# Up projection of a ConvGLU layer: eight column pairs by seven products of quadrants in place of eight (Strassen)

## The reference, cut to what matters

```python
u = jnp.einsum('bsd,df->bsf', x, w_up[l])
u_gate, u_val = jnp.split(u, 2, axis=-1)
a = jax.nn.gelu(causal_depthwise_conv(u_gate, w_conv[l], b_conv[l]), approximate=False) * u_val
ffn = jnp.einsum('bsf,fd->bsd', a, w_down[l])
x = layer_norm(DEEPNORM_ALPHA * x + ffn, ln2_g[l], ln2_b[l])
```

## Time and profile before

| what | value |
|---|---|
| median of 3 runs | 750.19 us (749.51 to 750.6) |
| the profiled execution | 750.42 us |
| its span | 748.6 us, mean granted clock 0.997 |
| PE busy | 736.8 us (98%), 3475 matmuls |
| PEld busy | 615.6 us (82%) |
| DVE, ACT, POOL busy | 361.7, 325.4, 336.5 us |

### The profile page before, as it was taken

The page is one execution under the profiler, slowest core; times in us unless marked ns, Lnnn a source line. Parts: engine busy times, 40 slices in busy tenths (PEclk is TensorE's granted clock), DMA queues, the critical chain, the costliest instruction groups (busy, mean ns, idle before and its releaser), DMA issues.

```text
span 748.6 us, 9524 instructions
## 1 busy us (share of the span) xinstructions
PE 736.8 (98%) x3475; PEld 615.6 (82%) x3475; DVE 361.7 (48%) x551; ACT 325.4 (43%) x439; POOL 336.5 (45%) x244
## 2 busy tenths in 40 slices
PE   9999999999999999999999999999999999999995
PEld 6888888788888888888898888888888888888884
DVE  3339589789789764455642211221221122322567
ACT  4325775775775775661123322333233233423410
POOL 6645343433424444991015454544445452755800
PEclk9999999999999999999999999999999999999998
DMA  8333314214124214670003222232323227232002
GB/s 306 105 113 111 115 57 121 76 57 137 61 84 113 85 57 157 236 252 29 0 2 134 91 92 104 84 112 84 111 85 101 95 91 289 98 112 84 29 28 84
DMA packets 24477, 78.32 MB, mean 105 GB/s; under 512 B 2944, under 2 KB 3328, under 8 KB 24448
## 3 DMA queue, kind: packets, MB, share of 16 engines
...
## 4 chain that ended last, share of the span: by engine, by line
PE 87%; DVE 6%; ACT 2%; issue 2%; DMA 1%; SPq 0%; DVEq 0%; ACTq 0%
PE ps L1035 86%; PE ps L1137 1%; DVE sb_t L847 1%; DMA fx_k<-k_bias_rows 1%; DVE fx_p L838 1%; DVE sb_t L878 1%; DVE sb_k L802 0%; ACT sb_hi L614 0%; DVE fx_p L875 0%; PE ps L1218 0%; DMA w_raw<-w_stream_in 0%; ACT w_hi L497 0%; DVE fx_lo L731 0%; DVE fx_k L731 0%; DVE q_bias_rows L791 0%
## 5 line engine op out<-in xcount | busy, mean ns | idle before, releaser
L430 POOL TENSOR_TENSOR w_lo<-w_raw,w_hi 128x512 fp32r<-128x512 f32 x218 | 292.4, 1363 | 368.5 <-ACT w_hi L497 362.5
L497 ACT ACTIVATE w_hi<-w_raw 128x1024 fp32r<-128x1024 f32 x108 | 114.3, 1058 | 212.4 <-DMA w_raw<-w_stream_in 212.2
L1035 PE MATMUL ps<-x1T_hi,w_hi 128*128 128x512 f32 (+1 forms) x376 | 141.3, 376 | 0.0
L1035 PE MATMUL ps<-x1T_lo,w_hi 128*128 128x512 f32 (+1 forms) x376 | 141.2, 375 | 0.0
L1035 PE MATMUL ps<-x1T_hi,w_lo 128*128 128x512 f32 (+1 forms) x376 | 141.2, 375 | 0.0
L998 DVE SCALAR_TENSOR_TENSOR conv<-ps,col,conv 128x511 f32<-128x511 f32 (+1 forms) x44 | 33.0, 749 | 166.8 <-ACT conv L694 163.8
L1035 PE MATMUL ps<-xT_hi,w_hi 128*128 128x512 f32 x264 | 105.2, 399 | 0.0
L1035 PE MATMUL ps<-xT_lo,w_hi 128*128 128x512 f32 x264 | 102.9, 390 | 0.0
L1035 PE MATMUL ps<-xT_hi,w_lo 128*128 128x512 f32 x256 | 100.0, 391 | 0.0
L1035 PEld LDWEIGHTS ps<-x1T_hi,w_hi 128*128 128x128 f32 x376 | 70.8, 188 | 12.9
L1035 PEld LDWEIGHTS ps<-x1T_lo,w_hi 128*128 128x128 f32 x376 | 70.8, 188 | 12.8
...
## 6 DMA issues: line engine op xcount, KB each, us to landing
w_raw<-w_stream_in SPq DMA_DIRECT2D x109, 512.0 KB, 3.3
...
```

What stands on the lines that cost most here:

```text
L430: lo = nc.gpsimd.tensor_tensor(w_lo[:, slot, cs], w_raw[:, slot, cs], plain(w_hi[:, slot, cs]), ALU.subtract)
L497: nc.scalar.activation(w_hi[:, slot, :], w_raw[:, slot, :], ACT.Copy).then_inc(hi_ready, 1)
L1035: return nc.tensor.matmul(out_, lhs, rhs, start=start, stop=stop, skip_group_check=True)
```

## The change

For f = 5, 7, ..., 19 (`S_FROM` = 2, `S_END` = 10: the odd member of pairs 2 to 9) the two weight blocks are taken as one matrix of 1024 features by 256 columns. It is cut in quadrants (`b11`, `b21` the halves of the gate block, `b12`, `b22` those of the up block), as is the input (512 features by 256 tokens), and the four quadrants of the result are made of seven products by Strassen's rule in place of eight. Each product has 4 x 3 matmuls of 256 columns.

- The sums of quadrants of the input (five, `s_raw`, with high and low parts `s_hi`, `s_lo`) are made once, at the start of the up stage: eleven additions of 1024 elements per partition on DVE, five copies on ACT, five subtractions on DVE.
- The sums of quadrants of the weight (five, `t_raw`) are made anew for each such f by `w_sums`: five additions of 512 elements on DVE, from the raw slots; the high parts by five copies on ACT, the low parts by five subtractions on POOL. Two products take a quadrant of the weight itself; for these ACT makes 512 columns of each block and POOL 512, in place of 1024 each.
- Products are accumulated in PSUM where the rule allows it. The rest is put together by a copy on ACT (`m_two`) and six additions of 256 elements on DVE; PE waits for the first of these (`m25_added`) before its fifth product, since that product overwrites what the addition reads.
- SP loads the next gate block only when the five sums are made. The f of even number and f = 0 to 3, 20, 21 are made as before.

```diff
+S_FROM, S_END = 2, FB // 2 - 1
+N_S = S_END - S_FROM
+T_ORDER = (1, 6, 3, 4, 7)
...
+        GATE_SLOT, UP_SLOT = (N_UP + 2) % 4, (N_UP + 3) % 4
+        C11, C21, C12, C22, M1 = (ps[:, c:c + HALF] for c in (1024, 1024 + HALF, 3 * 512, 5 * 512, 6 * 512))
+        def x_quarter(tile, keys, tokens):
+            return tile[:, 4 * keys:4 * keys + 4, HALF * tokens:HALF * (tokens + 1)]
...
-            with sp.Fori(0, n_loop) as i:
+            assert n_loop == S_END
+            for n in range(N_UP + 4, N_UP + 4 + 4 * S_FROM):
+                load_when_free(n)
+            with sp.Fori(S_FROM, S_END) as i:
                 for j in range(4):
                     sp.wait_ge(block_done, 4 * i + (N_UP + 1 + j))
+                    if j == 2:
+                        sp.wait_ge(t_summed, 5 * i + (5 - 5 * S_FROM))
                     load(4 * i + (N_UP + 4 + j), (N_UP + j) % 4)
...
+            with pool.Fori(S_FROM, S_END) as i:
+                pool.wait_ge(hi_ready, 4 * i + (N_UP + 3))
+                nc.gpsimd.tensor_tensor(w_hi[:, GATE_SLOT, 512:1024], w_raw[:, GATE_SLOT, 0:512],
+                                        plain(w_hi[:, GATE_SLOT, 0:512]), ALU.subtract).then_inc(lo_ready, 1)
+                pool.wait_ge(hi_ready, 4 * i + (N_UP + 4))
+                nc.gpsimd.tensor_tensor(w_hi[:, UP_SLOT, 0:512], w_raw[:, UP_SLOT, 512:1024],
+                                        plain(w_hi[:, UP_SLOT, 512:1024]), ALU.subtract).then_inc(lo_ready, 1)
+                for j, m in enumerate(T_ORDER):
+                    pool.wait_ge(t_hi_done, 5 * i + (j + 1 - 5 * S_FROM))
+                    nc.gpsimd.tensor_tensor(t_lo[m][:], t_raw[m][:], plain(t_hi[m][:]),
+                                            ALU.subtract).then_inc(t_split, 1)
+                for j in range(4, 6):
+                    low(4 * i + (N_UP + j), (N_UP + j) % 4)
...
+            def gated_up(f, j, ready, count):
+                act.wait_ge(ready, count)
+                act.wait_ge(act_ready, f + 1)
+                nc.scalar.activation(conv[:, j, :], bank(2 * j), ACT.Identity,
+                                     bias=col[:, ds(COL_CB + f, 1)],
+                                     scale=col[:, ds(f * CONV_WIDTH + (COL_CW + CONV_WIDTH - 1), 1)]
+                                     ).then_inc(cv_biased, 1)
+                act.wait_ge(cv_done, f + 1)
+                nc.scalar.activation(gelu[:, j, :], conv[:, j, :], ACT.Gelu).then_inc(gelu_done, 1)
+            def plain_up(f):
+                gated_up(f, f % 2, block_done, N_UP + 2 * f + 1)
...
+            def sums_high(ms):
+                for m in ms:
+                    act.wait_ge(s_summed, S_ORDER.index(m) + 1)
+                    nc.scalar.activation(s_hi[m][:], s_raw[m][:], ACT.Copy).then_inc(s_hi_done, 1)
...
+            high_in_order(N_UP + 3)
+            high_in_order(N_UP + 4)
+            sums_high(S_ORDER[:3])
+            plain_up(0)
...
+            with act.Fori(S_FROM, S_END) as i:
+                for g, (slot, own) in enumerate(((GATE_SLOT, slice(0, 512)), (UP_SLOT, slice(512, 1024)))):
+                    n = N_UP + 2 + g
+                    arrived(None, slot, i + n // 4)
+                    act.wait_ge(block_done, 4 * i + (n - 3))
+                    nc.scalar.activation(w_hi[:, slot, own], w_raw[:, slot, own], ACT.Copy).then_inc(hi_ready, 1)
+                for j, m in enumerate(T_ORDER):
+                    act.wait_ge(t_summed, 5 * i + (j + 1 - 5 * S_FROM))
+                    nc.scalar.activation(t_hi[m][:], t_raw[m][:], ACT.Copy).then_inc(t_hi_done, 1)
+                gated_up(2 * i, 0, block_done, 4 * i + (N_UP + 1))
+                act.wait_ge(block_done, 4 * i + (N_UP + 3))
+                nc.scalar.activation(m_two[:], C21, ACT.Copy).then_inc(m2_copied, 1)
+                for j in range(4, 6):
+                    n = N_UP + j
+                    high(None, n % 4, i + n // 4, 4 * i + (n - 3))
+                gated_up(2 * i + 1, 1, gate_done, i + (1 - S_FROM))
+            high_in_order(N_DOWN - 2)
+            high_in_order(N_DOWN - 1)
+            act.wait_ge(m7_done, N_S)
             a_high(0, 0)
             a_high(1, 1)
-            up_pair(FB // 2 - 1)
+            high_in_order(N_DOWN)
+            plain_up(FB - 2)
+            high_in_order(N_DOWN + 1)
+            high_in_order(N_DOWN + 2)
...
+            def times_halves(f, count):
+                dve.wait_ge(gelu_done, f + 1)
+                dve.wait_ge(up_done, count)
+                halves = ps[:, 3 * 512:7 * 512].rearrange("p (t c) -> p t c", t=2)[:, :, 0:HALF]
+                nc.vector.tensor_tensor(aT[:, ds(f, 1), :].rearrange("p o (t c) -> p (o t) c", t=2), halves,
+                                        gelu[:, 1, :].rearrange("p (t c) -> p t c", t=2),
...
+            def x_sum(m):
+                hi = lambda keys, tokens=0: blocks(plain(x_quarter(x1T_hi, keys, tokens)))
+                lo = lambda keys, tokens=0: blocks(plain(x_quarter(x1T_lo, keys, tokens)))
+                whole = blocks(s_raw[m][:])
+                steps = {2: ((turned(0), hi(1, 1), ALU.add), (whole, lo(1, 1), ALU.add)),
+                         5: ((hi(0), hi(1), ALU.add), (whole, lo(0), ALU.add), (whole, lo(1), ALU.add)),
+                         1: ((turned(1), hi(0), ALU.add), (whole, lo(0), ALU.add)),
+                         6: ((turned(0), hi(0), ALU.subtract), (whole, lo(0), ALU.subtract)),
+                         7: ((hi(1), turned(1), ALU.subtract), (whole, lo(1), ALU.add))}
+                for i, (a, b, op) in enumerate(steps[m]):
+                    done = sum(len(steps[n]) - 1 for n in S_ORDER[:S_ORDER.index(m)]) + i
+                    if i > 0:
+                        dve.wait_ge(s_part, done)
+                    nc.vector.tensor_tensor(whole, a, b, op).then_inc(
+                        s_part if i < len(steps[m]) - 1 else s_summed, 1)
+            def x_sum_low(m):
+                dve.wait_ge(s_hi_done, S_ORDER.index(m) + 1)
+                split_lo(s_lo[m][:], s_raw[m][:], s_hi[m][:]).then_inc(s_split, 1)
+            def w_sums(i):
+                for slot in (GATE_SLOT, UP_SLOT):
+                    dve.wait_ge(raw_in[slot], 16 * i + (16 * ((N_UP + 2 + (slot == UP_SLOT)) // 4) + 16))
+                b11, b21 = (w_raw[:, GATE_SLOT, 512 * k:512 * (k + 1)] for k in range(2))
+                b12, b22 = (w_raw[:, UP_SLOT, 512 * k:512 * (k + 1)] for k in range(2))
+                for m, a, b, op in ((1, b11, b22, ALU.add), (6, b11, b12, ALU.add), (3, b12, b22, ALU.subtract),
+                                    (4, b21, b11, ALU.subtract), (7, b21, b22, ALU.add)):
+                    nc.vector.tensor_tensor(t_raw[m][:], a, b, op).then_inc(t_summed, 1)
+            def first_products(i, count):
+                dve.wait_ge(m2_copied, count)
+                dve.wait_ge(block_done, 4 * i + (N_UP + 4))
+                nc.vector.tensor_tensor(m_sum[:], C12, m_two[:], ALU.add).then_inc(m25_added, 1)
+            def other_products(count):
+                dve.wait_ge(m25_added, count)
+                dve.wait_ge(m1_done, count)
+                nc.vector.tensor_tensor(m_both[:], M1, m_sum[:], ALU.subtract).then_inc(m1_less, 1)
+                dve.wait_ge(m1_less, count)
+                dve.wait_ge(m3_done, count)
+                nc.vector.tensor_tensor(m_up[:], C12, m_both[:], ALU.add).then_inc(m3_added, 1)
+                dve.wait_ge(m3_added, count)
+                nc.vector.tensor_tensor(C22, C22, m_up[:], ALU.add).then_inc(up_done, 1)
+                dve.wait_ge(m7_done, count)
+                nc.vector.tensor_tensor(m_gate[:], C21, m_both[:], ALU.add).then_inc(m4_added, 1)
+                dve.wait_ge(m4_added, count)
+                nc.vector.tensor_tensor(C11, C11, m_gate[:], ALU.add).then_inc(gate_done, 1)
             def a_low(f, slot):
                 dve.wait_ge(a_hi_done, f + 1)
                 split_lo(a_lo[:, slot, :], aT[:, ds(f, 1), :].rearrange("p o c -> p (o c)"),
                          a_hi[:, slot, :]).then_inc(a_split, 1)
-            with dve.Fori(0, FB // 2 - 1) as i:
-                up_pair(i)
+            dve.wait_ge(x1_split, 2 * SB)
+            for m in S_ORDER[:3]:
+                x_sum(m)
+            taps(0, 0)
+            x_sum_low(S_ORDER[0])
+            times_up(0, 0, block_done, N_UP + 2)
+            for m in S_ORDER[1:3]:
+                x_sum_low(m)
+            for m in S_ORDER[3:]:
+                x_sum(m)
+            taps(1, 1)
...
+            with dve.Fori(S_FROM, S_END) as i:
+                w_sums(i)
+                taps(2 * i, 0)
+                first_products(i, i + (1 - S_FROM))
+                times_up(2 * i, 0, block_done, 4 * i + (N_UP + 2))
+                other_products(i + (1 - S_FROM))
+                taps(2 * i + 1, 1)
+                times_halves(2 * i + 1, i + (1 - S_FROM))
             a_low(0, 0)
             a_low(1, 1)
-            up_pair(FB // 2 - 1)
...
```

(90 more changed lines are left out.)

63 lines of the change are left out of this document (29 added, 34 removed).

## The result

The changed kernel takes 769.98 us (median of 5 runs, 767.29 to 771.88), the kernel before 749.51 us (5 runs, 749.01 to 750.6, in the same job): ratio 1.0264, 95% interval 1.0248 to 1.028. The forecast was 763.5 us in a range of 749 to 769. The sign was right and the place was right; the size was too small by 6.5 us. The profiled execution of the changed kernel took 771.88 us with a span of 770.1, that of before 750.42 with 748.6. Its mean granted clock was 0.986 against 0.997.

A forecast was written before the change was run, and what follows sets the result against it. PE was taken to bound the up stage, so saved steps and waits count fully. -6.6 (products) + 13.3 (loop waits) + 6.5 (start) = +13.2 us on the kernel before gave 763.5 us, range 749 to 769.

The forecast's parts named there:

- seven products for eight: PE steps of eight odd f: 10.05 us each in place of 10.88, saving 0.83 us each, 6.6 in all.
- waits for `m_sum`: In every pair but the first PE starts the fifth product 1.9 us late: 7 x 1.9 = 13.3 us.
- clock behind them: PE's clock after the seven loop waits: no fall expected, nothing added to the sum.
- waits for `aT`: Start of the up stage: input sums make `aT` of f = 0 late by 1.6 us, f = 1 by 4.9; together 6.5.
- clock behind the longer one: After the 4.9 us wait the clock may fall, a further 1.5 us; left out of the sum, kept in the range.
- The waits of 1.9 us are shorter than 2.7.: Loop waits set against some 2.7 us of idleness before the clock fell at the program's end; no cost counted.
- The steps: PE matmuls in the up stage: 0.1197 us per 256 columns, 0.2267 per 512; 0.83 us saved per odd f.
- The rival by which loads bound the steps: If the 188 ns weight load were each step's price, +39 us, near 795 us; chance 0.02.
- Turns between DVE and POOL: Strict turns during the five weight sums: 1.27 us of POOL and 0.44 of DVE, 1.71 us a sum.
- The wait: PE's stand before the fifth product of a pair: it starts at 18.53 us in place of 16.63, 1.9 us late.
- The start: Input sums at the up stage's start cost 6.5 us; 2.5 without being held by POOL.
- The waits are longer, by the clock or by register work: 770: Rival: PE waits longer than forecast, through the clock or register work in the longer loop; 770 us, chance 0.07.

The follow-up runs named there:

- e1: Changed kernel with the five weight sums behind the taps of the even f and most input sums behind f = 0, 1 and 2: 743.81 us, ratio 0.991.
- e6: Changed kernel without POOL's five low parts of the weight sums, the high part multiplied twice instead: 749.59 us, ratio 0.999 to the kernel before.
- e2: Changed kernel with only the five weight sums moved behind the taps of the even f, start unchanged: 749.58 us, ratio 0.9994 to the kernel before.
- e4: Changed kernel with sixteen more 256-column matmuls, into a bank nobody reads, ahead of each wait for `m_sum`: 766.19 us, ratio 1.0209 to the kernel before.
- e5: Changed kernel with eight more 256-column matmuls, into a bank nobody reads, ahead of each wait for `m_sum`: 765.38 us, ratio 1.0212 to the kernel before.

## Why the prediction was wrong in size and right in kind

The account of the span's 21.5 us, with the distances of `m_sum` (20.95 us a pair without a wait in e1, 23.05 with one, 24.55 with a fall):

| part | forecast, us | measured, us |
|---|---|---|
| seven products for eight | -6.6 | 8 x (21.76 - 20.95) = -6.5 |
| waits for `m_sum` | 7 x 1.9 = +13.3 | 7 x (23.05 - 20.95) = +14.7 |
| clock behind them | 0 | 4 x 1.5 = +6.0 |
| waits for `aT` | 1.6 + 4.9 = +6.5 | 0.9 + 3.2 = +4.1 |
| clock behind the longer one | 0 (1.5 in the range) | +1.8 |
| up stage begins later | 0 | +1.2 |
| sum | +13.2 | +21.3 |

The last row but one lies ahead of the changed code. The first matmul on `x1T` is at 381.3 us in this run, at 380.1 before and in e1, and between 379.0 and 380.8 in the five others; I take it for scatter of the run. The errors in the two kinds of wait, +1.4 and -2.4 us, have opposite signs, so that the clock in the loop is nearly all of the miss.

**The step that failed** is the last sentence under the clock: "The waits of 1.9 us are shorter than 2.7." The 2.7 us were read from the end of the program, and I took them for the least idleness that lowers the clock. A single fall shows only that so much idleness was enough. The longest stand of PE in the trace of before was one of 1.6 us, at 133 us, with the clock at 1.00 behind it. So 1.9 us had no row, and zero was one end of its range, not its middle. With my own 1.5 us for a fall, the other end of this term was 7 x 1.5 = 10.5 us, and the range would have reached to 763.5 + 10.5 = 774. The clock was costed for the one long wait and not for the seven short ones, and the seven are the larger term: 6.0 us in the profiled execution. The Trainium skill (TensorE: Matmul & The Clock Gate, section Why this matters for your kernels) names an idle gap between bursts of matmuls that is to be avoided against throughput drops, and gaps of 2 us lie below it, so that by this row of its table the seven waits would have cost nothing beyond themselves. The trace does not agree: behind waits of 1.9 us the clock fell in four of seven cases, and the measurement decides.

**Point by point.**

- *The steps.* 256-column starts are 0.12 us apart with fresh weight loads, and the saving per pair is 0.81 us for the forecast's 0.83. The rival by which loads bound the steps is out.
- *Turns between DVE and POOL.* 1.71 us a sum forecast, 1.709 measured. It was put together from a POOL part of 1.27, read at 413.97 us in the up stage, and a DVE part of 0.44, read at 626.31 us in the down projection. That POOL and the order on DVE are both needed was argued ahead and is now shown (e6, e2). The Trainium skill (SBUF — State Buffer, section "Who interferes with whom") has a DVE instruction with two SBUF inputs contend with a POOL one that reads SBUF, by a lock on the ports that they share; e6 agrees, with 5.20 against 8.50 us.
- *The wait.* 1.9 us forecast, 1.85 by the list of waits, 2.0 by the starts, 2.1 by the length of a pair. The list of waits leaves out what surrounds a wait: the 0.16 us by which the last record outlasts its step, and the first start behind the wait, which took 0.22 us in place of 0.12. Against the forecast that is 0.2 us each, 1.4 us in all.
- *The start.* The sum of the two was 2.4 us too high (the rows below answer to the earlier trace rows). Both chains were sized from above: from the end of `x1T_lo` to that of `aT` of f = 0 I had 16.9 us and it took 16.1; from there to `aT` of f = 1, 15.8 and 14.3. In the second, four additions and two subtractions took 9.3 us where I had 10.3: POOL held up two of the six by 1.0 to 1.1 us each, not all a little. The rows:

```profile
405.00 0.68 DVE L1103 TENSOR_TENSOR aT<-ps,gelu 128x512 f32<-128x512 f32 x1
405.60 3.45 DVE L830 TENSOR_TENSOR s_lo<-s_raw,s_hi 128x1024 fp32r<-128x1024 f32 x2
408.97 1.21 DVE L1142 TENSOR_TENSOR s_raw<-ps,x1T_hi 128x1024 f32<-128x1024 f32 x1
410.22 2.32 DVE L1142 TENSOR_TENSOR s_raw<-s_raw,x1T_lo 128x1024 f32<-128x1024 f32 x1
...
419.30 0.68 DVE L1103 TENSOR_TENSOR aT<-ps,gelu 128x512 f32<-128x512 f32 x1
```

- *The clock at the start.* Behind the longer wait, for f = 3, the 512-column starts went to 0.43 us apart and the window reads 0.50; that was in the range and did come. It need not: behind the same wait of 3.1 us the clock fell in the traces of the changed kernel, e4 and e6, and stayed at 1.00 in those of e2 and e5. By the medians of e1 and e2, with no loop waits, the whole start costs 5.8 us, waits and clock.

```profile
420.04 0.50 PE L1230 MATMUL ps<-x1T_hi,w_hi 128*128 128x512 f32 x1 [3.08 <-DVE aT L1103]
...
421.72 0.63 PE L1230 MATMUL ps<-x1T_hi,w_lo 128*128 128x512 f32 x1
422.14 0.63 PE L1230 MATMUL ps<-x1T_hi,w_hi 128*128 128x512 f32 x1
...
422.00:423.00 1.00, 1.00 (x4) 0.71 (x3) 0.96 (x2) 0.00 (x0) 1.00 (x2) 0.50 0.00 0
```

- *The rivals.* "The waits are longer, by the clock or by register work: 770" is what came, and by its first half: the clock. I had given it 0.07, since it was no mechanism with a price but a remainder; that its figure was met is luck.
